# Seven half-size products for the gate projections of a two-block DiT kernel

## The chip, the cores and the metric

The kernel runs on one core of a Trainium2 chip. The metric is the device time of one execution in microseconds (us). The core has four compute engines with queues of their own: TensorE (PE, matmuls, with weight loads shown as PEld), VectorE (DVE), ScalarE (ACT) and GpSimd (POOL); SyncE (SP) here only issues DMAs. Engines meet through semaphores, and the whole order of the work is written out by hand.

## The reference

Two transformer blocks run one after the other over 256 context and 256 latent tokens, all in float32. The first part of the first block is a gated recurrence (HGRN2) with 16 heads of 128. Its projection is what the change touches:

```
def project(h):                                   # h: (tokens, 1024)
    q, i_in, f_fw, f_bw, z = jnp.split(h @ w_in, 5, axis=-1)   # w_in: 1024 x (5 * 2048)
    for d, g in enumerate((f_fw, f_bw)):
        log_f = logaddexp(log(lb), log1p(-lb) + log_sigmoid(g))  # lb is 0 for layer 0
        k = (1 - lb) * sigmoid(-g)
    return silu(q), i_in, gates, z
def readout(o, z):
    return (rmsnorm(o, o_gain) * silu(z)) @ w_out
```

With a lower bound of zero the forget gate f is sigmoid(g) and its key is sigmoid(-g). The recurrence itself runs both ways over the tokens, in chunks. After it `x = x + gate * rmsnorm(y)`, then an attention block, then the second transformer block with its feed-forward network.

## The kernel before

Activations lie with features on the partitions: `hT[:, k, t]` holds feature k*128+p of token t, with 512 columns, 256 of the context and 256 of the latents. `xT` is the residual stream in the same layout; between its normalization at the start and the end of the recurrence nobody reads or writes it.

The recurrence works through 8 pairs of heads. A **turn** of TensorE, `hg_turn_all(i)`, makes the projections of pair i and between them the core of pair i-1. There are five strips of weights a pair, each 1024 x 256, loaded into the slots of a ring by SyncE one turn ahead, in the order of `HG_ORDER = (2, 3, 0, 4, 1)`, which is f_fw, f_bw, q, z, v. A strip is used at idx = 2j and 2j+1, once for each of the two heads (m = 0, 1). `hg_project_tensor` (the matmul at L705) makes 8 matmuls of 128 x 512 for each, in PSUM bank idx % 2; a float32 matmul is two instructions in the trace, so a projection is 16 instructions of 512 columns. Strip 4 (v, L714) is made the other way round, tokens on the partitions.

Behind each projection `hg_core_after(i-1, idx)` runs a piece of the core: score matmuls of term 0 (L749) and of terms 1 to 7 (L752), at idx 7 transposes (L764), at idx 8 states (L776), at idx 9 outputs and means (L794, L800). Then `hg_mods_tensor` does part of a modulation projection for later blocks (L471) at idx 0, 2, 4 and 6.

The other engines, in the order of their own queues:

- ScalarE, for each idx: `hg_keys_scalar`, which packs the keys of the next term into K_c (L1507); then `hg_project_scalar`, which reads the projection out of PSUM: two sigmoids for f (L1489, L1490), one for q and z (L1496), a copy for v (L1498). At the end of a turn it takes squares and square roots (L1523, L1526).
- VectorE: `hg_scores_vector` for terms 0 to 7 (L1815 to L1830): it multiplies the keys and queries of the term (L1823, L1825: "merged"), copies the scores by a mask (L1828) and multiplies Tw (L1830). Between them stand two reciprocals of the pair before (L1864), its read-out (L1870, L1871) and from term 4 on the gating of q and z from PSUM (L1858, L1860). At the end come the states (L1841, L1844) and `hg_unpack_vector` (L1802 to L1807), which waits for the last outputs and sets up Qw, Kw and k_sum for the next pair ("unpacked").
- GpSimd: `move_pool`, once a turn, copies f and v (L2295, L2296: "moved").

TensorE's term t waits for K_c of that term (`kc_ready`), K_c for VectorE's product of the term before (`merged`), and that for the scores before it (`lv_full`). The first K_c of a pair waits for "unpacked".

The last pair's core runs beside the first part of the output projection (L1443). The second block's feed-forward network, further on, already uses Strassen's scheme (L1291): seven products of 4 matmuls of 256 columns a strip.

## Time and profile before

| | |
|---|---|
| median of 3 runs | 2645.95 us (2644.92 to 2647.23) |
| the profiled execution | 2646.15 us |
| its span, first to last instruction | 2644.4 us |
| mean granted TensorE clock | 0.988 |
| TensorE busy | 97% |
| VectorE, ScalarE, GpSimd busy | 40%, 22%, 7% |
| turns of the recurrence with an interleaved core | 7, from 117.8 us to 846.9 us |

A row of the timeline gives the start, the duration, the engine, the line, the operation with its output and inputs, the shapes, how many instructions are merged in the row, and in brackets the idle time before it with what ended it. A matmul row is some tenths longer than its share of the queue, since its end includes the drain; the distance from start to next start is what it costs. A wait inside a row is not shown as idle time.

### The profile page before, as it was taken

To read this page: it belongs to the slowest core of one execution; us is meant where nothing else is said; L and a number is where in the kernel's file an instruction comes from. 1 tells how busy PE (TensorE), PEld (TensorE's weight loads), DVE (VectorE), ACT (ScalarE), POOL (GpSimd) and SP (SyncE) were. 2 spreads that over 40 slices of the span, in tenths; PEclk is the share of its full clock that TensorE was granted. 3 is DMA by queue.
4 is the path that set the end of the run, shared out by engine and by line. 5 is a ranking of instruction groups with operands and counts; after the bars stand their busy time and mean duration, and the time that the engine had idled before them with its cause. 6 is when DMAs were issued, how large, how long until landed. Compare 5 with 4: busy or idle time off the path is not lost.

```text
span 2644.4 us, 31395 instructions
## 1 busy us (share of the span) xinstructions
PE 2557.8 (97%) x12728; PEld 1838.1 (70%) x12728; DVE 1067.6 (40%) x1883; ACT 574.6 (22%) x1118; POOL 175.9 (7%) x138
## 2 busy tenths in 40 slices
PE   7999999999999898899999999989999999998999
PEld 3556656656566576666886444678886587888998
DVE  2245365364464712254126111146664014115961
ACT  3112222122121112133224100121111013112211
POOL 0000000000000010000000000022120000003410
PEclk9999999999999998999999999999999999999999
DMA  8443343343424042212430122133333232344662
GB/s 314 159 159 131 124 143 111 127 159 114 140 96 112 9 142 80 70 38 71 119 94 9 59 68 63 64 96 91 84 102 88 66 80 64 104 150 129 175 170 70
DMA packets 319737, 280.58 MB, mean 106 GB/s; under 512 B 27617, under 2 KB 298601, under 8 KB 319513
## 3 DMA queue, kind: packets, MB, share of 16 engines
q1 hardware_dynamic: 317882, 274.89, 33.9%
q0 software_dynamic: 1280, 4.20, 0.4%
q8 instruction: 70, 1.15, 0.2%
q14 instruction: 26, 0.21, 0.0%
q10 hardware_dynamic: 479, 0.13, 0.0%
HBM read 278.15 MB, written 1.05 MB: 106 GB/s over the span
## 4 chain that ended last, share of the span: by engine, by line
PE 89%; DVE 7%; ACT 2%; issue 1%; DMA 1%; SPq 1%; ACTq 0%; DVEq 0%
PE ps L705 17%; PE ps L1291 11%; PE ps L1220 9%; PE ps L1363 4%; PE ps L714 4%; PE ps L1351 4%; PE ps L752 4%; PE ps L1232 3%; PE ps L1258 3%; PE ps L471 2%; PE ps L838 2%; PE ps L909 2%; PE ps L858 2%; DVE arena L2125 2%; PE ps L1064 2%; PE ps L794 1%
## 5 line engine op out<-in xcount | busy, mean ns | idle before, releaser
L705 PE MATMUL ps<-hT,ring_mem 128*128 128x512 f32 x1024 | 455.7, 598 | 1.7 <-ACT hT L484 1.7
L705 PEld LDWEIGHTS ps<-hT,ring_mem 128*128 128x128 f32 x1024 | 191.2, 191 | 234.9 <-issue 232.7
L1220 PE MATMUL ps<-hT,ring_mem 128*128 128x512 f32 (+1 forms) x768 | 250.3, 486 | 0.0
L1220 PEld LDWEIGHTS ps<-hT,ring_mem 128*128 128x128 f32 x768 | 145.9, 190 | 101.3 <-issue 91.4
L1291 PE MATMUL ps<-arena 128*128 128x256 f32 (+1 forms) x704 | 132.7, 332 | 13.8 <-DVE arena L2084 13.8
L2056 DVE TENSOR_TENSOR arena<-ps,arena 128x512 f32<-128x512 f32 (+1 forms) x48 | 26.8, 559 | 291.2 <-PE ps L1232 291.2
L752 PEld LDWEIGHTS ps<-arena,K_c 128*128 128x128 f32 x896 | 117.2, 196 | 32.6 <-issue 20.1
L1291 PE MATMUL ps<-hT,arena 128*128 128x256 f32 (+1 forms) x704 | 131.4, 330 | 0.0
L1291 PE MATMUL ps<-hT,ring_mem 128*128 128x256 f32 (+1 forms) x704 | 124.5, 330 | 4.2 <-DMA ring_mem<-in_w_up_dram 4.2
L1291 PEld LDWEIGHTS ps<-arena 128*128 128x128 f32 x704 | 111.8, 195 | 23.8 <-issue 14.3
L752 PE MATMUL ps<-arena,K_c 128*128 128x128 f32 x896 | 121.2, 290 | 7.4 <-ACT K_c L1507 7.3
L1291 PEld LDWEIGHTS ps<-hT,ring_mem 128*128 128x128 f32 x704 | 109.3, 194 | 14.1 <-DMA ring_mem<-in_w_up_dram 4.9
L423 DVE RECIPROCAL rstd<-root 128x256 f32<-128x256 f32 (+2 forms) x18 | 31.6, 1753 | 214.8 <-ACT root L396 214.8
L1351 PE MATMUL ps<-arena,ring_mem 128*128 128x512 f32 (+1 forms) x352 | 116.0, 491 | 2.1 <-DVE arena L2135 2.1
L1291 PEld LDWEIGHTS ps<-hT,arena 128*128 128x128 f32 x704 | 111.4, 194 | 9.5
L1363 PE MATMUL ps<-arena,ring_mem 128*128 128x256 f32 (+1 forms) x704 | 116.6, 327 | 0.0
L1363 PEld LDWEIGHTS ps<-arena,ring_mem 128*128 128x128 f32 x704 | 106.5, 191 | 10.1 <-issue 1.1
L714 PE MATMUL ps<-ring_mem,hT 128*128 128x256 f32 x512 | 113.0, 379 | 0.0
L2065 DVE SCALAR_TENSOR_TENSOR xT<-ps,mod_b,xT 128x256 f32<-128x256 f32 (+1 forms) x60 | 23.6, 427 | 216.2 <-PE ps L1351 88.3
L714 PEld LDWEIGHTS ps<-ring_mem,hT 128*128 128x128 f32 x512 | 96.1, 190 | 12.4
L1351 PEld LDWEIGHTS ps<-arena,ring_mem 128*128 128x128 f32 x352 | 67.7, 193 | 49.5 <-issue 41.4
L1507 ACT ACTIVATE K_c<-arena 128x1024 f32<-128x1024 f32 x56 | 64.0, 1143 | 170.9 <-DVE arena L1825 148.4
(278 smaller groups left out, 3668.0 us busy)
## 6 DMA issues: line engine op xcount, KB each, us to landing
ring_mem<-in_w_mod_dram SPq DMA_DIRECT2D x24, 2048.0 KB, 7.6
ring_mem<-in_w_up_dram SPq DMA_DIRECT2D x88, 512.0 KB, 5.2
ring_mem<-in_hg_w_in_dram SPq DMA_DIRECT2D x40, 1024.0 KB, 5.1
ring_mem<-in_w_in_dram SPq DMA_DIRECT2D x30, 1024.0 KB, 5.4
ring_mem<-in_w_down_dram SPq DMA_DIRECT2D x16, 1408.0 KB, 7.1
ring_mem<-in_ada_w_dram SPq DMA_DIRECT2D x8, 2048.0 KB, 7.7
ring_mem<-in_mla_w_in_dram SPq DMA_DIRECT2D x9, 1024.0 KB, 5.4
ring_mem<-in_hg_w_out_dram SPq DMA_DIRECT2D x8, 1024.0 KB, 12.0
```

Of the source, the lines that this page charges most:

```text
L471: mm = PE.matmul(bank[c * 32:c * 32 + 32, 0:256], sil_cols[:, cond * 16 + 2 * k:cond * 16 + 2 * k + 32], wm[:, k % 4, c * 256:c * 256 + 25 ...
L705: mm = PE.matmul(bank, wj[:, k, m * 128:m * 128 + 128], hT[:, k, :], start=k == 0, stop=k == 7)
L714: mm = PE.matmul(bank[:, g * 256:g * 256 + 256], hT[:, k, tok:tok + 128], wj[:, k, :], start=k == 0, stop=k == 7)
L752: mm = PE.matmul(dst, K_c[:, u * 128:u * 128 + 128], comb(Qw, 1 << (term - 1), u), start=True, stop=True)
L838: mm = PE.matmul(ps[:, 4 - 4 * h + j, 0:256], strip("hg_out", j, 16)[:, k, :], oz[:, k, h * 256:h * 256 + 256], start=k == 0, stop=k == 15)
L1220: mm = PE.matmul(ps[:, j, 0:n], wj[:, k, m * 128:m * 128 + 128], hT[:, k, c0:T], start=k == 0, stop=k == 7)
L1232: mm = PE.matmul(ps[:, 3 + j, 0:n], wj[:, k, m * 128:m * 128 + 128], brT[:, k, c0:T], start=k == k0, stop=k == k1 - 1)
L1258: mm = PE.matmul(ps[:, (0 if part == "_a" else 4) + j, m * (hi - lo):(m + 1) * (hi - lo)], wj[:, k, m * 128:m * 128 + 128], yT[:, k, c0 + ...
L1291: mm = PE.matmul(up_region(f, which, hw), left[:, k, :], right[:, k, 0:hw], start=k == 0, stop=k == 3)
L1351: mm = PE.matmul(ps[:, j, 0:n], wj[:, k, :], hid[:, k, 0:n], start=k == 0, stop=k == FT - 1)
L1363: mm = PE.matmul(ps[:, (4 if part == "_a" else 0) + j, 0:hi - lo], wj[:, k, :], hid[:, k, lo:hi], start=k == 0, stop=k == FT - 1)
L1507: S.activation(view(K_c, (2 * h, PC // (2 * h)), (h, 2), (1, h)), comb(Kw, h), ACT.Copy).then_inc(kc_ready, 1)
```

## The change

In turns 1 to 7 the four gate strips are no longer multiplied head by head. A strip A (1024 x 256 weights, as 2 x 2 blocks: feature half by head) and the activations B (feature half by token half) are multiplied by seven products of half the size, each 4 matmuls of 128 x 256. The first turn and the v strip stay as they were.

- Four sums of activations, T_hg, are made once, by VectorE in turn 0. They lie where xT lies. So xT is stored to a buffer in device memory first (`x_saved`), and loaded back after the last turn's fourth strip (`x_back`), ahead of the strips of the output projection; VectorE waits for it ahead of hg_post.
- Four sums of weights a strip: S1 and S3 by VectorE (`hg_sums_vector`, S3 in place), S2 and S4 by GpSimd (in place, after the products that need the old blocks).
- The seven products share the two PSUM banks 0 and 1, four regions of 256 columns, so that some have to be copied out before the next: ScalarE copies the first product of the sum P1, the seventh, the second and the fifth (`hg_one_scalar` and so on). VectorE adds them up in `hg_gather_vector`; the result ("whole") lies in SBUF.
- P1 and the two others lie over the states of the pair before (St), S1 and the whole z over its turned keys (kTw).
- The sigmoids and the gating now read the whole strip from SBUF, one strip later (`hg_signed_scalar`, `hg_read_gate_vector`, `hg_query_gate_vector`). The strips come in the order f_fw, z, q, f_bw, v.

```
-        HG_ORDER = (2, 3, 0, 4, 1)
+        HG_FIRST, HG_ORDER = (2, 3, 0, 4, 1), (2, 4, 0, 3, 1)
...
+            sp.wait_ge(x_copied, KT)
+            sp.dma_start(x_apart, xT.rearrange("p k t -> p (k t)")).then_inc(x_saved, 16)
...
+            sp.wait_ge(strips_used, (PAIRS - 1) * 5 + (hg_first + 4))
+            sp.wait_ge(x_saved, 16)
+            sp.dma_start(xT.rearrange("p k t -> p (k t)"), x_apart).then_inc(x_back, 16)
...
+        def hg_seven_tensor(pe, i, idx):
+            j, second = divmod(idx, 2)
+            a11, a12, a21, a22 = hg_parts(j)
+            one, six = ps[:, 0, 0:256], ps[:, 0, 256:512]
+            five, seven = ps[:, 1, 0:256], ps[:, 1, 256:512]
...
+            if not second:
+                ring.wait_loaded(pe, "hg_in", j, i)
+                if j == 0:
+                    pe.wait_ge(act_freed, i * 6 - 1)
+                else:
+                    pe.wait_ge(u_ready, nth(i, j - 1))
+                product(one, a11, hT[:, 0:4, 0:256]).then_inc(one_full, 1)
+                if j == 0:
+                    pe.wait_ge(act_freed, i * 6)
+                else:
+                    pe.wait_ge(whole_ready, nth(i, j - 1))
+                pe.wait_ge(s3_ready, nth(i, j))
+                product(seven, a21, T_hg[:, 2]).then_inc(seven_full, 1)
+                pe.wait_ge(one_kept, nth(i, j))
+                product(one, a12, hT[:, 4:8, 0:256]).then_inc(two_full, 1)
+                pe.wait_ge(seven_kept, nth(i, j))
+                product(seven, a22, T_hg[:, 3])
+                return
+            product(five, S1_hg, T_hg[:, 0]).then_inc(five_full, 1)
+            pe.wait_ge(two_kept, nth(i, j))
+            pe.wait_ge(s2_ready, nth(i, j))
+            product(six, a11, T_hg[:, 1]).then_inc(six_full, 1)
+            pe.wait_ge(five_kept, nth(i, j))
+            pe.wait_ge(s4_ready, nth(i, j))
+            strip_used(product(five, a12, hT[:, 4:8, 256:512]))
...
+        def hg_one_scalar(act, i, j):
+            act.wait_ge(one_full, nth(i, j))
+            if j == 0:
+                act.wait_ge(o_full, raised(i * 2 - 2))
+                act.wait_ge(unpacked, i)
+                act.wait_ge(moved, i)
+            else:
+                act.wait_ge(whole_ready, nth(i, j - 1))
+            S.activation(P1_hg, ps[:, 0, 0:256], ACT.Copy).then_inc(one_kept, 1)
...
-                    hg_project_scalar(act, i, idx)
+                    j = idx // 2
+                    if idx >= 8:
+                        hg_project_scalar(act, i, idx)
+                    elif idx % 2:
+                        hg_five_scalar(act, i, j)
+                    else:
+                        hg_one_scalar(act, i, j)
+                        if j:
+                            hg_signed_scalar(act, i, j - 1)
+                        hg_seven_scalar(act, i, j)
+                        hg_two_scalar(act, i, j)
                     if idx == 7:
+                        act.wait_ge(dve_freed, i * 4 + 2)
                         hg_turn_scalar(act, i - 1)
+                        hg_signed_scalar(act, i, 3)
...
+        def hg_gather_vector(dve, st, i, j):
+            dve.wait_ge(one_kept, nth(i, j))
+            dve.wait_ge(two_kept, nth(i, j))
+            V.tensor_tensor(hg_part(j, 0, 256), hg_part(j, 0, 256), P1_hg, ALU.add)
+            dve.wait_ge(six_full, nth(i, j))
+            V.tensor_tensor(P1_hg, P1_hg, ps[:, 0, 256:512], ALU.add).then_inc(u_ready, 1)
+            dve.wait_ge(u_ready, nth(i, j))
+            dve.wait_ge(seven_kept, nth(i, j))
+            dve.wait_ge(five_kept, nth(i, j))
+            st.link(V.tensor_tensor(hg_part(j, 256, 512).rearrange("p (s t) -> p s t", s=2), view(P1_hg, (0, 2), (1, 256)),
+                                    P57_hg.rearrange("p (s t) -> p s t", s=2), ALU.add))
+            st.mark(V.tensor_tensor(hg_part(j, 768, 256), hg_part(j, 512, 256), P57_hg[:, 0:256], ALU.add))
+            dve.wait_ge(strips_used, ring.stages["hg_in"]["first"] + i * 5 + (j + 1))
+            st.settle()
+            V.tensor_tensor(hg_part(j, 256, 512), hg_part(j, 256, 512), ps[:, 1, :], ALU.add).then_inc(whole_ready, 1)
+            if j < 3:
+                hg_sums_vector(dve, st, i, j + 1)
...
+                    if gates and term % 2:
+                        hg_gather_vector(dve, st, i + 1, term // 2)
...
             with pool.Fori(1, PAIRS) as i:
+                for j in range(4):
+                    a11, a12, _, _ = hg_parts(j)
+                    pool.wait_ge(s3_ready, nth(i, j))
+                    pool.wait_ge(one_kept, nth(i, j))
+                    nc.gpsimd.tensor_tensor(a11, S1_hg, a11, ALU.subtract).then_inc(s2_ready, 1)
+                    pool.wait_ge(two_kept, nth(i, j))
+                    pool.wait_ge(s2_ready, nth(i, j))
+                    nc.gpsimd.tensor_tensor(a12, a12, a11, ALU.subtract).then_inc(s4_ready, 1)
                 move_pool(pool, i)
```

How TensorE's queue reads at the start of a turn. A matmul here is one row entry where the trace has two instructions. Before (L705 the projection, L749 and L752 scores):

```order
L705 MATMUL ps<-hT,ring_mem 128x512 x8
L740 ISA
L749 MATMUL ps<-arena 128x128 x8
L742 ISA
L745 ISA
L752 MATMUL ps<-arena,K_c 128x128 x4
```

And now, with the waits of each (L721 a product, L816 and L819 scores):

```order
L721 MATMUL ps<-hT,ring_mem 128x256 [waits act_freed]
L721 MATMUL ps<-hT,ring_mem 128x256 x3
L734 ISA [waits act_freed]
L721 MATMUL ps<-xT,ring_mem 128x256 [waits s3_ready]
L721 MATMUL ps<-xT,ring_mem 128x256 x3
L721 MATMUL ps<-hT,ring_mem 128x256 [waits one_kept]
L721 MATMUL ps<-hT,ring_mem 128x256 x3
L721 MATMUL ps<-xT,ring_mem 128x256 [waits seven_kept]
L721 MATMUL ps<-xT,ring_mem 128x256 x3
L807 ISA [waits unpacked]
L816 MATMUL ps<-arena 128x128 [waits rt_ready]
```

The wait on one_kept stands in the middle of the first strip, ahead of all scores, where before nothing stood between the strip's start and its end.

ScalarE's queue at the start of a turn, before (L1507 K_c, L1489 and L1490 the sigmoids of f):

```order
L1507 ACT_TABLE_LOAD
L1507 ACTIVATE K_c<-arena 128x1024 [waits unpacked]
L726 ISA
L1489 ACT_TABLE_LOAD [waits moved,unpacked]
L1489 ACTIVATE arena<-ps 128x512 [waits proj_full]
L1490 ACTIVATE arena<-ps 128x512
```

And now (L1622 K_c, L1585 the copy of the first product, L1589 of the seventh, L1595 of the second, L1604 and L1606 the sigmoids of f over the whole strip):

```order
L1622 ACT_TABLE_LOAD
L1622 ACTIVATE K_c<-arena 128x1024 [waits unpacked]
...
L1585 ACTIVATE arena<-ps 128x256 [waits moved,unpacked,o_full]
L1589 ACTIVATE arena<-ps 128x256 [waits seven_full]
L1595 ACTIVATE arena<-ps 128x256 [waits two_full]
...
L1622 ACTIVATE K_c<-arena 128x1024 [waits merged]
L1585 ACTIVATE arena<-ps 128x256 [waits whole_ready,one_full]
L1604 ACT_TABLE_LOAD
L1604 ACTIVATE arena<-arena 128x1024 [waits whole_ready]
...
L1606 ACTIVATE arena<-arena 128x1024 [waits act_freed]
L1589 ACTIVATE arena<-ps 128x256 [waits seven_full]
```

The table load and the sigmoids of strip 0 have moved into strip 1, between the copy of its first product and that of its seventh.

## Rows read from the trace of the kernel before

**Rows 1.** The page, busy time by engine and the chain that ended last.
```profile
PE 2557.8 (97%) x12728; PEld 1838.1 (70%) x12728; DVE 1067.6 (40%) x1883; ACT 574.6 (22%) x1118; POOL 175.9 (7%) x138
...
PE 89%; DVE 7%; ACT 2%; issue 1%; DMA 1%; SPq 1%; ACTq 0%; DVEq 0%
```
**Rows 2.** Timeline of TensorE in two steady turns: start, duration, line, operation.
```profile
221.97 7.03 PE L705 MATMUL ps<-hT,ring_mem 128*128 128x512 f32 x16
...
326.12 7.03 PE L705 MATMUL ps<-hT,ring_mem 128*128 128x512 f32 x16
332.98 1.95 PE L749 MATMUL ps<-arena 128*128 128x128 f32 x16
334.82 2.92 PE L752 MATMUL ps<-arena,K_c 128*128 128x128 f32 x16
337.67 1.93 PE L471 MATMUL ps<-ring_mem,sil_cols 128*32 128x256 f32 x32
339.53 7.13 PE L705 MATMUL ps<-hT,ring_mem 128*128 128x512 f32 x16
346.50 2.08 PE L752 MATMUL ps<-arena,K_c 128*128 128x128 f32 x16
```
**Rows 3.** Timeline of TensorE in the feed-forward stage, the starts of two strips, one after the other.
```profile
1810.83 3.62 PE L1291 MATMUL ps<-hT,ring_mem 128*128 128x256 f32 x16
...
1822.92 3.62 PE L1291 MATMUL ps<-hT,ring_mem 128*128 128x256 f32 x16
```
**Rows 4.** Timeline of VectorE at the start of the turn of 326.12.
```profile
324.68 2.29 DVE L1802 TENSOR_TENSOR arena<-arena 128x2048 f32<-128x2048 f32 x1 [9.96 <-PE ps L794]
...
337.77 2.22 DVE L1825 TENSOR_TENSOR arena<-arena 128x1024 f32<-128x1024 f32 x1
...
342.41 3.35 DVE L1864 RECIPROCAL root<-root 128x512 f32<-128x512 f32 x1
345.68 1.16 DVE L1823 TENSOR_TENSOR arena<-arena 128x1024 f32<-128x1024 f32 x1
```
**Rows 5.** Timeline of ScalarE at the start of the same turn.
```profile
331.87 1.51 ACT L1507 ACTIVATE K_c<-arena 128x1024 f32<-128x1024 f32 x1 [2.90 <-DVE arena L1807]
333.40 1.28 ACT L1489 ACT_TABLE_LOAD   x1
334.69 0.60 ACT L1489 ACTIVATE arena<-ps 128x512 f32<-128x512 f32 x1
...
349.88 1.06 ACT L1507 ACTIVATE K_c<-arena 128x1024 f32<-128x1024 f32 x1 [2.10 <-DVE arena L1825]
```
**Rows 6.** Timeline of all engines in the feed-forward stage, one strip.
```profile
1847.90 0.69 DVE L2143 TENSOR_TENSOR arena<-ring_mem 128x512 f32<-128x512 f32 x1
1848.50 0.41 DVE L2108 TENSOR_TENSOR arena<-root,ps 128x256 f32<-128x256 f32 x1
1848.73 1.27 POOL L2334 TENSOR_TENSOR arena<-arena,ring_mem 128x512 f32<-128x512 f32 x1 [9.45 <-DVE arena L2143]
...
1859.38 0.39 ACT L1706 ACTIVATE root<-ps 128x256 f32<-128x256 f32 x1 [2.09 <-PE ps L1291]
```
**Rows 7.** Timeline of TensorE in the last pair's core, rows behind gaps.
```profile
868.71 3.49 PE L752 MATMUL ps<-arena,K_c 128*128 128x128 f32 x16 [2.07 <-ACT K_c L1507]
...
876.53 2.05 PE L752 MATMUL ps<-arena,K_c 128*128 128x128 f32 x16 [0.70 <-ACT K_c L1507]
...
883.45 2.05 PE L752 MATMUL ps<-arena,K_c 128*128 128x128 f32 x16 [1.44 <-ACT K_c L1507]
```
**Rows 8.** Windows there: stretch, length, TensorE's busy time, granted clock, DMA share, GB/s.
```profile
869.00:872.00 3.00, 3.00 (x17) 0.51 0.00 0
```
**Rows 9.** Timeline of VectorE in turn 0.
```profile
79.89 0.69 DVE L1858 TENSOR_TENSOR arena<-ps,arena 128x512 f32<-128x512 f32 x1 [43.52 <-ACT arena L1496]
```
**Rows 10.** The page, DMA issues: count, size, median time to landing.
```profile
ring_mem<-in_w_mod_dram SPq DMA_DIRECT2D x24, 2048.0 KB, 7.6
```
**Rows 11.** Timeline of SyncE's issues at the last turn's end.
```profile
815.17 11.71 SPq L130 DMA_DIRECT2D ring_mem<-in_hg_w_out_dram  x4
```

More of the change, by code:

```diff
@@ L167, in build @@
         xT = sb("xT", KT * T).rearrange("p (k t) -> p k t", k=KT)
+        T_hg = xT.rearrange("p k t -> p (k t)").rearrange("p (s k t) -> p s k t", s=4, k=4)
+        x_apart = nc.dram_tensor("x_apart", (128, KT * T), F32, kind="Internal").ap()
         hT = sb("hT", KT * T).rearrange("p (k t) -> p k t", k=KT)
@@ L543, in strip_load @@
             def strip_load(i, j):
-                sp.dma_start(strip("hg_in", j, 8), wk["hg_w_in"][0][:, :, bass.ds(i * 256 + HG_ORDER[j] * 2048, 256)]
+                order = HG_FIRST if isinstance(i, int) and i == 0 else HG_ORDER
+                sp.dma_start(strip("hg_in", j, 8), wk["hg_w_in"][0][:, :, bass.ds(i * 256 + order[j] * 2048, 256)]
                              ).then_inc(loaded[j], 16)
@@ L680, in hg_mods_tensor, with nth, hg_parts, product @@
                 mod_turn_tensor(pe, mod_number(i, s_), mod_bank(s_))
+        def nth(i, j):
+            return i * 4 + (j - 3)
+        def hg_parts(j):
+            wj = strip("hg_in", j, 8)
+            return wj[:, 0:4, 0:128], wj[:, 4:8, 0:128], wj[:, 0:4, 128:256], wj[:, 4:8, 128:256]
+        def hg_seven_tensor(pe, i, idx):
[3 more added lines that the diff above has]
+            five, seven = ps[:, 1, 0:256], ps[:, 1, 256:512]
+            def product(dst, left, right):
+                for k in range(4):
+                    mm = PE.matmul(dst, left[:, k, :], right[:, k, :], start=k == 0, stop=k == 3)
+                return mm
+            if not second:
[23 more added lines that the diff above has]
+            strip_used(product(five, a12, hT[:, 4:8, 256:512]))
         def hg_project_tensor(pe, i, idx):
@@ L1498, in hg_project_scalar, with hg_part, hg_seven_scalar, hg_two_scalar @@
                 S.activation(v_st[:, 2 * m:2 * m + 2, :], bank, ACT.Copy).then_inc(act_freed, 1)
+        hg_whole = (f_st[:, 1, :], z_hg, q_st, f_st[:, 0, :])
+        def hg_part(j, at, n):
+            return hg_whole[j][:, at:at + n]
+        def hg_one_scalar(act, i, j):
[4 more added lines that the diff above has]
+                act.wait_ge(moved, i)
+            else:
+                act.wait_ge(whole_ready, nth(i, j - 1))
+            S.activation(P1_hg, ps[:, 0, 0:256], ACT.Copy).then_inc(one_kept, 1)
+        def hg_seven_scalar(act, i, j):
+            act.wait_ge(seven_full, nth(i, j))
+            S.activation(P57_hg[:, 256:512], ps[:, 1, 256:512], ACT.Copy).then_inc(seven_kept, 1)
+        def hg_two_scalar(act, i, j):
+            act.wait_ge(two_full, nth(i, j))
+            if j == 2:
+                act.wait_ge(lv_full, i * 16 - 14)
+            S.activation(hg_part(j, 0, 256), ps[:, 0, 0:256], ACT.Copy).then_inc(two_kept, 1)
+        def hg_five_scalar(act, i, j):
+            act.wait_ge(five_full, nth(i, j))
+            S.activation(P57_hg[:, 0:256], ps[:, 1, 0:256], ACT.Copy).then_inc(five_kept, 1)
+        def hg_signed_scalar(act, i, j):
+            act.wait_ge(whole_ready, nth(i, j))
+            if j in (0, 3):
+                S.activation(k_st[:, 1 - j // 3, :], hg_whole[j], ACT.Sigmoid, scale=-1.0).then_inc(act_freed, 1)
+                act.wait_ge(act_freed, i * 6 + (2 * (j // 3) + 1))
+                S.activation(hg_whole[j], hg_whole[j], ACT.Sigmoid).then_inc(act_freed, 1)
+                return
+            if j == 1:
+                act.wait_ge(o_ready, raised(i * 2 - 2))
+            for m in range(2):
+                if j == 2:
+                    act.wait_ge(dve_freed, i * 4 + (m + 1))
+                S.activation(sg[:, m, :], hg_part(j, m * T, T), ACT.Sigmoid).then_inc(sig_ready, 1)
         def hg_keys_scalar(act, i, term):
@@ L2202, in _ @@
             modulate_coef(st, mod_a[0][:, 8:16, :], vecs[:, PRE:PRE + 8])
+            hg_turned_vector(dve)
             for idx in range(4, 8):
@@ L2208, in _, with core @@
             hg_unpack_vector(dve, st, 0)
-            def core(i, gates, first=False):
+            hg_sums_vector(dve, st, 1, 0)
+            def core(i, gates, first=False, more=True):
                 hg_scores_vector(dve, st, i, 0)
@@ L2217, in core @@
                         hg_read_vector(dve, st, i - 1)
+                    if gates and term % 2:
+                        hg_gather_vector(dve, st, i + 1, term // 2)
                     if gates and term == 4:
                         hg_mods_vector(dve, i + 1, 0)
-                    if gates and term >= 4:
-                        hg_gate_vector(dve, i + 1, term)
+                        for m in range(2):
+                            hg_read_gate_vector(dve, i + 1, m)
+                    if gates and term == 6:
+                        for m in range(2):
+                            hg_query_gate_vector(dve, i + 1, m)
                 if gates:
@@ L2225, in core @@
                 if gates:
+                    if more:
+                        hg_sums_vector(dve, st, i + 2, 0)
                     hg_unpack_vector(dve, st, i + 1)
             core(0, True, True)
-            with st.loop(2, PAIRS - 1, LEVELS + 4) as i:
+            with st.loop(2, PAIRS - 1, LEVELS + 16) as i:
                 core(i - 1, True)
-            core(PAIRS - 2, True)
+            core(PAIRS - 2, True, more=False)
             core(PAIRS - 1, False)
```

64 lines of the change are left out of this document (50 added, 14 removed).

## The prediction

> **What bounds the kernel now.** I read the page's busy line and chain first. TensorE is busy for 97% of the span and holds 89% of the chain that ended last, VectorE 7% [rows 1]. So work taken from TensorE counts in full, as long as nothing makes it wait. Then I took one steady turn of the head-pair loop on TensorE's timeline [rows 2]: the same projection matmul starts at 221.97 and at 326.12, so a turn is 104.15 us. Its instructions stand end to end, and the weight strips are there in time. The reader should see in these rows what the seven-microsecond first projection does: while it runs, VectorE unpacks the last pair and ScalarE makes the first K_c. Last I read those two engines at the start of the turn [rows 4, 5], the stage of this same kernel that already runs Strassen products [rows 3, 6], and the rows after TensorE's longer gaps [rows 7, 8].
>
> The profiled execution took 2646.15 us (span 2644.4 and 1.75 around it), 0.2 us above the median of 2645.95, so I work from 2646.15. No change that this kernel's measurement can tell is under about 0.2% (5.3 us).
>
> **What is removed.** In turns 1 to 7 each of four strips has two projections of 16 instructions of 512 columns. One takes 6.97 us from start to next start after the modulation matmuls (339.53 to 346.50) and 6.87 after scores (the next at 348.42 runs so); together 13.84 us [rows 2]. Seven products take 12.09 us a strip in the feed-forward stage (1810.83 to 1822.92) and so 1.73 each, weight loads hidden [rows 3]. The saving is 1.75 a strip, 7.0 a turn, 49 over seven turns. Taken alone that gives 2597.
>
> **What the first strip of a turn waits for.** I set the start of the turn to 0, which is 326.12. Before, ScalarE read the first projection only at 7.1, so its needs were met. Now the third product waits for one_kept, ScalarE's copy of the first product. That copy stands behind three things: unpacking by VectorE, the v and f move by GpSimd, and, in ScalarE's own queue, the first K_c. Unpacking starts when the last outputs are done, at -1.44 (324.68) [rows 4], and ends at 5.7; K_c runs from 5.75 to 7.26 (331.87, 1.51 long) [rows 5]. The copy adds 0.39 (a copy of 256 columns in the stage with Strassen) [rows 6]. TensorE has two products before it, to 3.45, and can go on at about 7.7. That is a new gap of 4.2 us, in each of turns 2 to 7, since nothing in this chain is made shorter. In turn 1 unpacking is long done and the move and first K_c set the end; I take 0.7 there.
>
> **What the second strip waits for.** The remaining two products run to 11.15. Scores 0 and 1 take 1.84 and 2.85 (332.98 to 334.82 to 337.67 [rows 2]), and end at 15.85. VectorE's step of term 1 then follows: the Q product ends 2.3 later (2.22 long, 337.77), the masked copies and the product on Tw take 2.4 to the start of a reciprocal at 342.41, and that 3.35 [rows 4]. It is then 24.0. Only behind these does its gather of strip 0 stand: three adds of 0.41 and one of 0.69, then the 0.69 that reads the last products, then 0.69 twice for the weight sums of strip 1 [rows 6]. With the handovers it is ready at 27.9. TensorE is through mods, three products, scores 2 and the next strip's first product at 26.5: a gap of 1.4. Then the copy of the first product stands on ScalarE behind K_c for term 3, which needs term 2 merged by VectorE (about 1.2 for each of two products after the sums [rows 4], then 1.06 for K_c [rows 5] and 0.39): copy done at 31.6, TensorE there at 29.7, a gap of 1.9. Next ScalarE has the sigmoids of the finished strip ahead of the copy of the seventh product, two of 1024 elements at about 1.0 each, and the table load of 1.28 that used to stand at the turn's start [rows 5] and now stands here. Copy done at 35.2, TensorE at 33.4: 1.8 to 1.9. The same bookkeeping for strips 2 and 3 gives 1.1 (a queue of hg_read and the gather on VectorE, with K_c 5 behind) and 0.6 (K_c 7). Together 7.0 in strips 1 to 3.
>
> So a steady turn gets 4.2 + 7.0 = 11.2 of waits for 7.0 of products: +4.2. Turn 1 has no reciprocals and no unpacking in the way; its waits come to 4.1, so it is 2.9 shorter. Over the stage: 6 x 4.15 - 2.9 = +22.
>
> **What a gap costs besides itself.** After a gap of 2.07 us that ended at 868.71 the granted clock fell to 0.51 in 869 to 872 [rows 7, 8], the lower of the two levels (1.2 GHz): 16 instructions took 3.49 instead of the 2.05 that the same ones take after a gap of 0.70 [rows 7], and the stretch of 3 us and some tenths at half speed is worth 1.5 to 1.7 us. The gap of 4.2 is twice as long, with as little in front of it as two products, so I count 1.7 for each of six turns: +10. For the gaps of 1.4, 1.9 and 1.9 I count nothing more: a slower product there mostly eats the wait for ScalarE that follows it; the upper end takes another 1.7 a turn. The Trainium skill ("TensorE: Matmul & The Clock Gate", "HAM oscillation — how this bites in real kernels") says that a loop whose short bursts are broken by waits falls back to the half clock in every turn, and the trace agrees at this gap; by that rule the case to reckon with is the one where the second strip's gaps do it too.
>
> **The other edits.** VectorE gets 5 adds and 2 sums a strip, 3.4 us, 13.7 a turn; it is 40% busy [rows 1], and this costs only where it is named above. Four sums of 1024 elements in turn 0, about 1.2 each, stand in an idle time of 43.5 us before 79.89 [rows 9]; the store of 2 MB they wait for takes about the 7.6 us of a load of that size [rows 10] and is issued near 42: nothing, and if it took 30 us more, still nothing. GpSimd's two differences a strip (1.27 beside VectorE's adds, which stay at 0.41 [rows 6]) have the scores and modulation matmuls, about 5 us, as cover: nothing; at twice the time still nothing. VectorE's sums for the next turn's first strip lie in its idle time before unpacking (9.96 us [rows 4]). The load back and, behind it, the strips of the output projection start 20 us later than before (815.17 [rows 11]), about 25 us before their first use; 7.6 and some 12 us for them fit. If not, up to 5 us, once. Against all this the lower bound of the waits is the 4.2 gap alone (its chain has a row for each step); the other 7.0 rest on laying the three queues beside each other, and I bound them by 2 and 12 a turn.
>
> The table load is the other place where page and row differ. The row shows 1.28 and the next activation 1.29 after it started [rows 5]. The Trainium skill ("ScalarE: Activation LUTs", "What ACT_TABLE_LOAD costs") counts a drain besides, 2.66 us together; by it the third gap of strip 1 would be 1.4 longer and the sum, as an estimate from that page, 8 us higher. I keep the row.
>
> Sum: 2646 + 22 + 10 = 2678.
>
> **The rivals.**
> *Only the first gap counts.* If VectorE and ScalarE stay ahead in strips 1 to 3 (it needs the gather to come before TensorE's second product of the next strip, thus 1.4 us found, and K_c 3 earlier by 1.9), a turn is 7.0 - 4.2 - 1.7 = 1.1 shorter, turn 1 6.3: 2646 - 13 = 2633. For it: VectorE idles half of the turn. Against: its work of terms 1 and 2 is packed, with both reciprocals and slow strided products. It turns to slower where the waits of strips 1 to 3 pass 1.1 a turn. Chance 0.09.
> *Clock falls twice a turn.* The second strip's gaps bring the clock down as well, with a cost that reaches the five products behind them, or the 4.2 gap brings two slow stretches: 1.7 more in each of six or seven turns, 2690. For: three gaps with 1.73 of work between them. Against: a gap of 1.44 left the 2.05 of the matmuls behind it as it was [rows 7]. Chance 0.22.
> *The gaps leave the clock alone* and the waits are as laid: 2668. Against it stands what followed the gap of 2.07 [rows 7, 8]. Chance 0.12.
> *The products don't come at 1.73*, as weights now come from sums in place: the same kind of operand runs at 1.73 in the other stage [rows 3], so 0.02; about 2690.
> *Net nothing*: waits smaller by a third: 2646 to 2655. Chance 0.07.
> The forecast, the waits as laid and one slow stretch a turn, has the remaining 0.48; its own range is 2667 to 2688. The range for 8 in 10 is 2652 to 2698. Faster by over 0.2%: 0.09. Within 0.2%: 0.05. Slower: 0.86.
>
> **What would show it.** On TensorE a steady turn of about 110 us, with a gap of about 4 us, released by ScalarE's copy of 256 columns, after two products; the granted clock at 0.5 right behind it. Gaps of 1 to 2 us in strip 1, released by VectorE's subtraction on ring_mem and by ScalarE's copies, the latter behind a table load. The first turn near 101 to 102. Products at 1.73. No idle time at the first output strips and none before hg_post. I am wrong if steady turns come below 104, if the largest gap is not the one at the turn's start, or if GpSimd's differences release TensorE.

## The result, and the profile after

| | before | after |
|---|---|---|
| median of 4 runs each, us | 2646.38 (2644.92 to 2647.23) | 2685.13 (2683.56 to 2687.28) |
| ratio after / before | | 1.0149, 95% interval 1.0133 to 1.0164 |
| the profiled execution: time, span, us | 2646.15, 2644.4 | 2683.56, 2681.8 |
| mean granted clock of TensorE | 0.988 | 0.983 |

The change makes the kernel 39 us slower. The forecast was 2678, its own range 2667 to 2688.

The page of the kernel after, busy time and the chain that ended last, to be laid beside [rows 1]:
```profile
PE 2533.0 (94%) x13400; PEld 1969.3 (73%) x13400; DVE 1194.6 (45%) x2083; ACT 607.3 (23%) x1202; POOL 266.1 (10%) x194
...
PE 74%; DVE 14%; issue 9%; ACT 3%; DMA 0%; DVEq 0%; POOL 0%; ACTq 0%; SPq 0%; POOLq 0%
```
TensorE is busy for 25 us less, and the span is 37 us longer, so it stands idle for some 62 us more. Its share of the chain that ended last falls from 89% to 74%. VectorE's rises from 7% to 14%, and that of "issue", time in which an engine waited for nothing that the profile shows, from 1% to 9%.

What TensorE waits for from 100 to 880 us, after (waiting tensor and line, releaser, us in total, times, longest):
```profile
PE ps L721 <- ACT arena L1585: 44.3, 28, 4.0
PE ps L721 <- ACT arena L1589: 12.1, 7, 1.7
PE ps L721 <- DVE ring_mem L1996: 6.3, 6, 1.1
PE ps L831 <- ACT arena L1633: 1.8, 7, 0.3
```
L721 is the product of the new projections. L1585 is ScalarE's copy of the first product, L1589 that of the seventh, L1996 VectorE's sum of weights. Before, only the last row's wait was there in these turns (2.1 in all). The sum of the first three is 62.7 us in 41 waits.

TensorE's timeline after, one steady turn's first strips and the next turn's start (start, duration, line, operation, in brackets the idle time before and its releaser); it answers [rows 2]:
```profile
330.31 1.89 PE L721 MATMUL ps<-hT,ring_mem 128*128 128x256 f32 x8
332.04 1.89 PE L721 MATMUL ps<-xT,ring_mem 128*128 128x256 f32 x8
337.90 3.78 PE L721 MATMUL ps<-hT,ring_mem 128*128 128x256 f32 x8 [3.97 <-ACT arena L1585]
341.47 2.74 PE L721 MATMUL ps<-xT,ring_mem 128*128 128x256 f32 x8
344.05 1.95 PE L816 MATMUL ps<-arena 128*128 128x128 f32 x16
...
360.74 1.99 PE L721 MATMUL ps<-xT,ring_mem 128*128 128x256 f32 x8 [1.05 <-DVE ring_mem L1996]
364.37 1.99 PE L721 MATMUL ps<-hT,ring_mem 128*128 128x256 f32 x8 [1.64 <-ACT arena L1585]
368.10 1.99 PE L721 MATMUL ps<-xT,ring_mem 128*128 128x256 f32 x8 [1.73 <-ACT arena L1589]
...
385.52 1.99 PE L721 MATMUL ps<-hT,ring_mem 128*128 128x256 f32 x8 [0.95 <-ACT arena L1585]
...
404.10 1.99 PE L721 MATMUL ps<-hT,ring_mem 128*128 128x256 f32 x8 [0.59 <-ACT arena L1585]
...
441.95 1.89 PE L721 MATMUL ps<-hT,ring_mem 128*128 128x256 f32 x8
```
Product follows product at 1.73 (330.31 to 332.04), as in the stage that had them before [rows 3]. This turn takes 111.64, against 104.15. The seven turns start at 117.45, 219.84, 330.31, 441.95, 552.4, 663.9 and 775.98, and the last ends at 886.62: 102.39, then 110.5, 111.6, 110.4, 111.5, 112.1 and 110.6.

The windows at the end of the first gap of that turn and behind it (stretch, length, busy time, granted clock, DMA share, GB/s), for [rows 8]:
```profile
337.00:338.00 1.00, 0.10 (x1) 0.50 0.00 0
338.00:342.00 4.00, 4.00 (x10) 0.50 0.00 0
342.00:344.00 2.00, 2.00 (x8) 0.71 0.00 0
344.00:356.00 12.00, 12.00 (x91) 1.00 0.34 113
```
The clock falls while TensorE still stands idle (1.00 from 334 to 336, 0.67 from 336 to 337), is at its lower level, 1.2 GHz, when the copy is done, and stays there for some 5 us behind the gap of 3.97. The two products there take 3.57 and 2.58 from start to start instead of 1.83 and 1.73: 2.6 us lost.

Why the copy is late is seen on VectorE and ScalarE, as in [rows 4, 5]. VectorE's timeline after, at the turn's start:
```profile
328.87 2.29 DVE L1929 TENSOR_TENSOR arena<-arena 128x2048 f32<-128x2048 f32 x1 [8.62 <-PE ps L861]
...
334.83 1.21 DVE L1934 TENSOR_TENSOR arena<-arena 128x1024 f32<-128x1024 f32 x1
...
353.49 3.35 DVE L2038 RECIPROCAL root<-root 128x512 f32<-128x512 f32 x1
...
359.99 0.69 DVE L1996 TENSOR_TENSOR ring_mem<-ring_mem 128x512 f32<-128x512 f32 x1
```
ScalarE's timeline in the same stretch:
```profile
336.07 1.50 ACT L1622 ACTIVATE K_c<-arena 128x1024 f32<-128x1024 f32 x1 [2.90 <-DVE arena L1934]
337.48 0.37 ACT L1585 ACTIVATE arena<-ps 128x256 f32<-128x256 f32 x1
...
362.99 1.06 ACT L1622 ACTIVATE K_c<-arena 128x1024 f32<-128x1024 f32 x1 [9.98 <-DVE arena L1952]
363.95 0.37 ACT L1585 ACTIVATE arena<-ps 128x256 f32<-128x256 f32 x1
364.33 1.28 ACT L1604 ACT_TABLE_LOAD   x1
365.63 1.06 ACT L1604 ACTIVATE arena<-arena 128x1024 f32<-128x1024 f32 x1
...
367.68 0.36 ACT L1589 ACTIVATE arena<-ps 128x256 f32<-128x256 f32 x1
```
Each copy that TensorE needs takes 0.37 and stands behind something long that doesn't concern it: at 337.48 behind the unpacking and the first K_c, at 363.95 behind K_c of term 3, at 367.68 behind a table load and two sigmoids. VectorE's sum of weights (359.99) stands behind the gather, and that behind a reciprocal of 3.35.

Part of the unpacking ahead of 337.48 is long because two engines copy at once. At 118.31, with VectorE idle, GpSimd's two copies of the move take 1.89 and 1.04, and at 107.25, with GpSimd idle, VectorE's two copies of the unpacking take 0.69 each. In this turn both run together from 328.88 on: VectorE's take 2.38 and 1.52, GpSimd's 4.03 and 1.50. So some 2.5 us of the chain ahead of the first K_c come with this overlap. It is there in the kernel before too, where the first projection covers it; no run here took it away.

### The profile page after: what moved, and what is told of

It is laid out like the page before. It is cut to its first block, busy times and chain, and to the rows that moved or that the text cites. A ratio compares the mean times of both kernels' runs of the same rounds, so it can differ in the third digit from the quotient of the medians.

```text
span 2681.8 us, 33406 instructions
## 1 busy us (share of the span) xinstructions
PE 2533.0 (94%) x13400; PEld 1969.3 (73%) x13400; DVE 1194.6 (45%) x2083; ACT 607.3 (23%) x1202; POOL 266.1 (10%) x194
## 4 chain that ended last, share of the span: by engine, by line
PE 74%; DVE 14%; issue 9%; ACT 3%; DMA 0%; DVEq 0%; POOL 0%; ACTq 0%; SPq 0%; POOLq 0%
PE ps L1358 11%; PE ps L1287 9%; PE ps L721 7%; PE ps L1430 4%; PE ps L1418 4%; PE ps L781 4%; PE ps L1299 3%; PE ps L1325 3%; PE ps L905 2%; PE ps L976 2%; PE ps L925 2%; DVE arena L1952 2%; PE ps L819 2%; DVE arena L2299 2%; PE ps L1131 2%
## 5 line engine op out<-in xcount | busy, mean ns | idle before, releaser
L1287 PEld LDWEIGHTS ps<-hT,ring_mem 128*128 128x128 f32 x768 | 145.9, 190 | 101.3 <-issue 91.4
L721 PE MATMUL ps<-hT,ring_mem 128*128 128x256 f32 x672 | 171.7, 401 | 44.3 <-ACT arena L1585 44.3
L721 PEld LDWEIGHTS ps<-hT,ring_mem 128*128 128x128 f32 x672 | 130.2, 200 | 75.3 <-ACT arena L1585 55.6
L721 PE MATMUL ps<-xT,ring_mem 128*128 128x256 f32 x672 | 163.0, 386 | 18.5 <-ACT arena L1589 12.1
L721 PEld LDWEIGHTS ps<-xT,ring_mem 128*128 128x128 f32 x672 | 129.3, 194 | 41.7 <-ACT arena L1589 15.0
L1358 PE MATMUL ps<-arena 128*128 128x256 f32 (+1 forms) x704 | 132.7, 332 | 13.9 <-DVE arena L2258 13.9
L1622 ACT ACTIVATE K_c<-arena 128x1024 f32<-128x1024 f32 x56 | 64.0, 1143 | 353.9 <-DVE arena L1952 331.3
L819 PE MATMUL ps<-arena,K_c 128*128 128x128 f32 x896 | 119.0, 287 | 7.4 <-ACT K_c L1622 7.3
L819 PEld LDWEIGHTS ps<-arena,K_c 128*128 128x128 f32 x896 | 115.1, 192 | 14.6 <-ACT K_c L1622 11.7
L1358 PEld LDWEIGHTS ps<-hT,ring_mem 128*128 128x128 f32 x704 | 109.2, 193 | 13.8 <-DMA ring_mem<-in_w_up_dram 4.5
L1430 PEld LDWEIGHTS ps<-arena,ring_mem 128*128 128x128 f32 x704 | 106.5, 191 | 10.1 <-issue 1.1
## 6 DMA issues: line engine op xcount, KB each, us to landing
ring_mem<-in_hg_w_out_dram SPq DMA_DIRECT2D x8, 1024.0 KB, 12.1
```

What stands on the lines that cost most here:

```text
L721: mm = PE.matmul(dst, left[:, k, :], right[:, k, :], start=k == 0, stop=k == 3)
L819: mm = PE.matmul(dst, K_c[:, u * 128:u * 128 + 128], comb(Qw, 1 << (term - 1), u), start=True, stop=True)
L1287: mm = PE.matmul(ps[:, j, 0:n], wj[:, k, m * 128:m * 128 + 128], hT[:, k, c0:T], start=k == 0, stop=k == 7)
L1358: mm = PE.matmul(up_region(f, which, hw), left[:, k, :], right[:, k, 0:hw], start=k == 0, stop=k == 3)
L1430: mm = PE.matmul(ps[:, (4 if part == "_a" else 0) + j, 0:hi - lo], wj[:, k, :], hid[:, k, lo:hi], start=k == 0, stop=k == FT - 1)
L1622: S.activation(view(K_c, (2 * h, PC // (2 * h)), (h, 2), (1, h)), comb(Kw, h), ACT.Copy).then_inc(kc_ready, 1)
```

## The experiments

In all of them names are those of the kernel after. An edit can move the line numbers by a few: the second sum of weights, L1996, is L2000, L2001 or L2005 in some runs, and the copy of the first product, L1585, is L1588 in one. A ratio is to the kernel before, run on the same chip in the same set (its medians there 2645.1 to 2645.5).

**One part alone: the products.** The kernel before with its two projections of a strip in turns 1 to 7 made as seven products of 4 x 256 columns, with no sums, differences, copies or extra waits; part of the gate projections is left out by that.
```
-            for n ... k in range(8): matmul over 512 columns      (two projections, 32 instructions)
+            for n in range(4 - m):                                 (m = 0, 1: 4 + 3 products)
+                for k in range(4):
+                    mm = PE.matmul(bank[:, n % 2 * 256:n % 2 * 256 + 256], wj[...], hT[...], start=k == 0, stop=k == 3)
```


> The kernel before, with each projection of turns 1 to 7 made of 4 (first head) or 3 (second head) products of 4 matmuls of 256 columns in place of 8 of 512; no sums, no copies, no store of the residual stream. It leaves out part of the gate projections. It is the price of the seven products with nothing to wait for. My theory: 12.09 us a strip instead of 13.84, 49 us less in all, 2597 (2594 to 2601). Rival (weight loads of 0.19 us show beside matmuls of 0.22, or the shorter projections uncover waits for K_c): 2610 or more.

Measured: 2597.01, ratio 0.9817 (0.9801 to 0.9834). The prediction's first term alone gave 2597. Of the 48 us some 46 are in the turns, which take 97.56 against 104.15, so 6.6 a turn instead of 7.0. The rest lies in the last pair's core, 63.8 us long against 65.5, where the clock fell at other places. So the whole 88 us between 2597 and 2685 is what the scheme costs around its products.

**One part alone: the residual stream's trip to memory.** The kernel before plus the store of xT, VectorE's wait for it, the load back and the wait for that.
```
+            sp.dma_start(x_apart, xT.rearrange("p k t -> p (k t)")).then_inc(x_saved, 16)
...
+            dve.wait_ge(x_saved, 16)
...
+            sp.dma_start(xT.rearrange("p k t -> p (k t)"), x_apart).then_inc(x_back, 16)
...
+            dve.wait_ge(x_back, 16)
```


> The kernel before with only the store of the residual stream to device memory after its fourth strip load, the wait of VectorE for it in turn 0, the load back ahead of the output projection's strips, and VectorE's wait for that; nothing writes over xT. My theory: nobody waits for either, within 0.1% of the kernel before, 2643 to 2649. Rival (2 MB ahead of the output projection's strips make TensorE wait at its first use): 2650 or more.

Measured: 2644.48, ratio 1.0001 (0.9992 to 1.001). It costs nothing that can be measured. What the products lose is lost within the turns.

**The first gap taken away.** Strip 0's first and fifth product are kept in sg, which is free then, and no longer in the buffer that unpacking fills. So both copies can go ahead of the first K_c, and the waits for unpacking and the move go to the copy of the second product.
```
-        P1_hg, P57_hg = St_flat[:, 0:256], St_flat[:, 256:768]
+        P1_of = lambda j: sg_flat[:, 0:256] if j == 0 else St_flat[:, 0:256]
...
-                act.wait_ge(unpacked, i)         (in hg_one_scalar, j == 0)
+                act.wait_ge(dve_freed, i * 4)
...
+                    if idx == 0:                 (ahead of hg_keys_scalar)
+                        hg_one_scalar(act, i, 0)
+                        hg_seven_scalar(act, i, 0)
```


> The changed kernel, with the products of strip 0 kept in sg, which is idle then, so that ScalarE copies the first and the seventh product at once and ahead of the first K_c; only the copy of the second product waits for unpacking. My theory (the gap at a turn's start is the chain unpacking, K_c, copy, and it costs a slow stretch of the clock besides): the gap of 4.1 us (start 332.04 to 337.90 less a product) and 1.6 us of slow clock go in six turns, 0.7 in the first, nothing comes back: steady turns of 105.5 to 106 instead of 111.5, 2649 us in all (2643 to 2656). Rival (VectorE, packed with terms 1 and 2, sets the pace, and the time comes back as longer gaps in strip 1): above 2670.

Measured: 2645.73, ratio 1.0001 (0.9991 to 1.001); turns of 104.9 to 105.0. TensorE's timeline at the turn's start has no gap and no slow product:
```profile
326.60 1.89 PE L723 MATMUL ps<-hT,ring_mem 128*128 128x256 f32 x8
328.32 1.89 PE L723 MATMUL ps<-xT,ring_mem 128*128 128x256 f32 x8
...
346.94 1.99 PE L723 MATMUL ps<-xT,ring_mem 128*128 128x256 f32 x8 [1.11 <-DVE ring_mem L2005]
350.57 1.99 PE L723 MATMUL ps<-hT,ring_mem 128*128 128x256 f32 x8 [1.64 <-ACT arena L1585]
354.30 1.99 PE L723 MATMUL ps<-xT,ring_mem 128*128 128x256 f32 x8 [1.74 <-ACT arena L1589]
```
The first gap was worth 39 us. The turns are 6.2 shorter than the kernel after's 111.1 (the mean of turns 2 to 7), of which the gap's idle time is 4.0, its restart 0.26 (below), and the rest, some 2.0, fits the slow clock, which is gone from behind it. The edit changes the buffer and the order of the copies at once, so it doesn't say which of the two would have been enough. The other waits stayed as they were, and by themselves they eat the whole saving of the products.

**The waits of strips 1 to 3 taken away.** There both copies go ahead of the term's K_c, and the sigmoids go last. Strip 0 stays as in the kernel after.
```
+                    if idx in (2, 4, 6):         (ahead of hg_keys_scalar)
+                        hg_one_scalar(act, i, j)
+                        hg_seven_scalar(act, i, j)
...
                         hg_two_scalar(act, i, j)
+                        if j:
+                            hg_signed_scalar(act, i, j - 1)
```


> The changed kernel, with ScalarE's copies of the first and seventh product of strips 1 to 3 ahead of K_c, and the sigmoids of the finished strip last of the idx. The gap at the turn's start stays. My theory (the gaps in strips 1 to 3 come from the order in ScalarE's queue): of the gaps of strip 1 only the one that VectorE's sums end (1.05) is left, and about 0.8 before strip 2's second product; 5.5 us a steady turn, 3.5 in the first: 2649 (2642 to 2657). Rival (K_c, now later, holds up the scores by as much): 2670 or above.

Measured: 2656.16, ratio 1.0042 (1.0026 to 1.0059), 29 us below the kernel after. That misses my 2649, though it is inside the range given: a steady turn is 4.0 us shorter (107.1 against 111.1), not 5.5, and the first one 3.9. TensorE's timeline shows what stayed and what came:
```profile
331.14 3.45 PE L721 MATMUL ps<-hT,ring_mem 128*128 128x256 f32 x8 [3.97 <-ACT arena L1585]
...
365.79 1.99 PE L721 MATMUL ps<-hT,ring_mem 128*128 128x256 f32 x8 [0.20 <-ACT arena L1599]
...
372.84 1.99 PE L721 MATMUL ps<-xT,ring_mem 128*128 128x256 f32 x8 [1.18 <-DVE ring_mem L2000]
```
Three waits for L1585 and one for L1589 are gone from each turn, and a new one for VectorE's sum has come in the third strip (12 such waits, 13.6 us over the stage, against 6 and 6.3). L1599, the copy of the fifth product, holds it up by 0.2. TensorE, arriving earlier, finds the next late engine.

**Only the sigmoids moved.** The table load and the sigmoids go behind the copies, while K_c stays ahead of them.
```
                         hg_one_scalar(act, i, j)
-                        if j:
-                            hg_signed_scalar(act, i, j - 1)
                         hg_seven_scalar(act, i, j)
                         hg_two_scalar(act, i, j)
+                        if j:
+                            hg_signed_scalar(act, i, j - 1)
```


> The changed kernel, with ScalarE's sigmoids of the finished strip, and the table load ahead of them, behind the copies of the seventh and second product; K_c stays ahead of the first copy. My theory: the gap of 1.74 before strip 1's fourth product goes and nothing else: 1.9 to 2.0 in each of seven turns, 2671 (2666 to 2676). Rival (the sigmoids, later, hold up the copy of the fifth product or the gating): 2680 or more.

Measured: 2668.12, ratio 1.0092 (1.0077 to 1.0107), 17 us below the kernel after. What TensorE waits for from 100 to 870 us:
```profile
PE ps L721 <- ACT arena L1585: 44.3, 28, 4.0
PE ps L721 <- DVE ring_mem L1996: 6.4, 6, 1.1
...
```
The row of L1589 is gone, the others are as they were. That row was 12.1 us in 7 waits; with 0.26 for each restart (below) it is worth 13.9, or 2.0 a turn. The steady turns are shorter by 1.9 (109.3 against 111.1). In the profiled executions the seven turns together are 13.2 shorter (755.98 against 769.17), which the wait and its restart cover. The other 3 us of the 17 lie elsewhere: the kernel before was itself 1.3 faster in this set (2645.08 against 2646.38), and the stretch behind the last turn, which the edit doesn't touch, takes from 1791.5 to 1798.1 in the profiled executions of all these kernels.

**Strip 1's gaps as one chain.** The gather of strip 0 goes ahead of the first reciprocal, in VectorE's order. If gaps add up one by one, 1.05 of 9.9 goes and the kernel gets faster. If the reciprocal only moves ahead of term 2, K_c 3 comes later instead.
```
+                    if gates and term == 1:
+                        hg_gather_vector(dve, st, i + 1, 0)
...
-                    if gates and term % 2:
+                    if gates and term in (3, 5, 7):
```


> The changed kernel, with VectorE's first reciprocal of a turn behind the gather of strip 0 instead of ahead of it. My theory (the three gaps of strip 1 are one chain: VectorE's queue up to merged of term 2, then K_c, then the copy): the gap of 1.05 that VectorE's sums end goes, but merged of term 2 comes 0.8 later since VectorE now idles for the strip's last product before its gather, so the gap before the third product grows by 1.05 + 0.26 + 0.5 or so; a steady turn 0.3 to 0.8 longer, 2688 (2684 to 2692). Rival (each gap has its own cause and taking one away gains it): 1.3 less a turn, 2677.

Measured: 2691.55, ratio 1.018 (1.0166 to 1.0194): slower than the kernel after by 6 us, by 8 if the ratios are compared. A steady turn is 1.6 longer (112.7 against 111.1), where 0.3 to 0.8 was expected. Its VectorE and then its TensorE:
```profile
357.73 0.69 DVE L1996 TENSOR_TENSOR ring_mem<-ring_mem 128x512 f32<-128x512 f32 x1
358.34 3.35 DVE L2038 RECIPROCAL root<-root 128x512 f32<-128x512 f32 x1
```
```profile
359.76 1.89 PE L721 MATMUL ps<-xT,ring_mem 128*128 128x256 f32 x8
365.31 3.78 PE L721 MATMUL ps<-hT,ring_mem 128*128 128x256 f32 x8 [3.66 <-ACT arena L1585]
369.04 3.03 PE L721 MATMUL ps<-xT,ring_mem 128*128 128x256 f32 x8
```
The sum of weights is in time (359.76 follows with no idle). The gap of 1.05 is now part of the next one, which grows from 1.64 to 3.66, and behind that the products run at half speed: 3.73 and 2.86 from start to start. The slow products also cover the wait for L1589, which is gone from the steady turns. A turn has 0.8 less idle time and 0.5 less for two restarts, and 2.9 more for the slow products (3.73 and 2.7 to 2.9 instead of 1.83 and 1.73), a term that the expectation didn't have. So the gap that was closed came back in the next one, in the same chain from the end of scores 1 to K_c 3, and one long gap cost more here than two short ones, since the clock fell.

**What the clock costs.** Two products that nobody reads, of the same operands as the third, go between the second and third product of strip 0, into a free bank. They do 3.45 us of useless work in the 4 us gap, and in turn 1, where the gap is 0.67, they are mostly extra work.
```
+                if j == 0:
+                    for _ in range(2):
+                        product(ps[:, 2, 0:256], a12, hT[:, 4:8, 0:256])
```


> The changed kernel with two useless products of 4 matmuls of 256 columns (3.45 us of work whose result nobody reads, in PSUM bank 2) at the start of each turn, between the first two products and the wait for the copy. More work in the same gap. My theory (a gap costs the wait and a slow stretch of the clock behind it): the idle time falls from 4.0 to about 0.5 in six turns, the granted clock stays up there, each steady turn is about 1.6 us shorter, the first turn 2.8 longer: about 7 us less than the changed kernel, 2678 (2674 to 2682). Rival (the slow matmuls behind the gap, 3.4 to 3.6 for 1.83, come from the wait itself or from the operands): as the changed kernel or 3 us more, 2685 to 2688.

Measured: 2675.02, ratio 1.0115 (1.01 to 1.0131). With more work, the kernel is 10 us faster than the kernel after (9 by the ratios).
```profile
334.41 3.62 PE L721 MATMUL ps<-hT,ring_mem 128*128 128x256 f32 x16
338.54 1.99 PE L721 MATMUL ps<-hT,ring_mem 128*128 128x256 f32 x8 [0.52 <-ACT arena L1588]
340.37 1.89 PE L721 MATMUL ps<-xT,ring_mem 128*128 128x256 f32 x8
```
From the turn's first product (330.95) to the third product's start it is 7.59, to the hundredth what the kernel after shows (330.31 to 337.90). So the copy comes when it did, and what changed is the speed behind it: 1.83 and 1.73 for the two products, with a granted clock of 1.00 from 335 to 344. The six steady turns are 2.1 shorter each (109.0 against 111.1), and the first is 2.5 longer (104.9 against 102.4); together that is the 10 us. So the slow clock cost 2.1 a steady turn, more than the 1.6 expected and the 1.7 of the prediction.

The Trainium skill ("TensorE: Matmul & The Clock Gate", "HAM oscillation — how this bites in real kernels") tells of short bursts of matmuls, each followed by a wait for a DMA, after each of which the clock is down again. The waits here are for another engine's copy. The clock was down behind each of the six first gaps of 3.8 to 4.0 us, and behind none of the gaps of strip 1.

**All together.** The two orders of copies, and the last pair's read behind the gather of strip 1 instead of ahead of it.
```
-                    if idx in (2, 4, 6):
+                    if idx in (0, 2, 4, 6):      (copies ahead of K_c in every strip)
...
-                    if not first and term == 3:
-                        hg_read_vector(dve, st, i - 1)
                     if gates and term % 2:
                         hg_gather_vector(dve, st, i + 1, term // 2)
+                    if not first and term == 3:
+                        hg_read_vector(dve, st, i - 1)
```


> Both edits of e1 and e2 together, and VectorE's read-out of the last pair after the gather of strip 1. My theory: of the waits of a turn only the 1.05 before strip 1's second product is left, a steady turn of about 99.5 to 100: 2646 less 49 for the products plus about 10 for what is left = 2607 (2600 to 2614), below the kernel before. Rival (VectorE's longer queue, 66 us of work a turn, becomes the bound once TensorE's waits are gone): 2625 or more.

Measured: 2611.08 (2608.62 to 2613.43), ratio 0.9868 (0.9852 to 0.9885); turns of 100.4. This version beats both kernels: 35 us faster than before, 74 faster than after. From the expectation's 2607 it is 4 off. What TensorE still waits for, from 200 to 800 us, in this run (the copies of the fifth product are L1603 here):
```profile
PE ps L723 <- DVE ring_mem L2001: 6.7, 6, 1.2
PE ps L821 <- ACT K_c L1626: 4.0, 6, 0.7
...
PE ps L723 <- ACT arena L1603: 0.9, 5, 0.2
```
The first is the sum of weights behind the reciprocal, the second K_c. With 0.26 for each of 17 restarts the three rows make 16.0 in six turns, 2.7 a turn; the turn is 2.8 above the 97.56 of the products alone. The moved read was not run alone, so its share is not known.

## Why the prediction was right

*The saving.* 1.73 a product: right. Worked out 7.0 a turn, measured 6.6 (products alone): the product behind the modulation matmuls takes 1.83 up to the next start, as the projection there took 6.97 instead of 6.87. I had left that 0.10 out of the new side.

*The gap at the turn's start.* Predicted 4.2, with a restart at 7.7 from the turn's start. Measured: a restart at 7.59, 4.13 after the point where the third product would have begun (two of 1.73). The cause, a copy behind unpacking and the first K_c, was right, and taking it away brought back 39 us. In turn 1, 0.7 was predicted and 0.67 is there.

*Strips 1 to 3.* Predicted 1.4, 1.9, 1.8 to 1.9, 1.1 and 0.6, each with its releaser. From start to start they are 1.21, 1.80, 1.89, 1.11 and 0.75, with those releasers (the idle rows plus 0.16, next point): 6.8, against 7.0.

*What a wait costs beside its idle row.* A product starts 1.73 after the one before, but its record is 1.89 long; idle time is counted from the record's end, so it leaves out 0.16. The product behind a wait then takes 1.83 up to the next start. Together 0.26 a wait, 10.6 over 41 waits. My terms, made from start to start, held the 0.16 and not the 0.10, which is 4 us over the 41 waits.

*The clock.* Predicted 1.7 for each of six turns, from the rows behind another gap [rows 7, 8]. That it falls was right; the size was low. Behind the first gap of turns 2 to 7 the two products lose 1.6, 2.6, 1.4, 2.5, 3.0 and 1.6, in all 12.7 or 2.1 a turn. The first of them:
```profile
227.25 3.60 PE L721 MATMUL ps<-hT,ring_mem 128*128 128x256 f32 x8 [3.80 <-ACT arena L1585]
230.69 1.89 PE L721 MATMUL ps<-xT,ring_mem 128*128 128x256 f32 x8
```
(230.69 - 227.25 is 3.44, less 1.83.) Filling the gap gave the same 2.1 a steady turn. The rival with a second fall in each turn did not come: behind the gaps of strip 1 the products take 1.99. Its total of 2690 is nearer to the measured 2685 than the forecast, but by a mechanism that the rows don't show. Where one gap there was made 3.66 long, in the run with the gather ahead, the clock did fall.

*The sum.* The turn from 330.31 to 441.95: -6.6 for products, +9.9 idle, +1.6 for six restarts, +2.6 for the clock, together +7.5, and 111.64 - 104.15 is 7.5. Turn 1: -6.6 + 3.6 idle + 1.3 for five restarts is -1.7, and 102.39 - 104.15 is -1.8. All seven turns are 40 us longer (769.2 against 729.1), where the prediction had 32 (22 for waits and products, 10 for the clock): the products saved 3 less, the 0.10 of the restarts makes 4, the clock nearly 3, and the gaps were laid 2 too long. In the rest of the kernel the profiled execution is 2.7 faster, mostly in the last core, and its 2683.56 is 1.6 below the median. That makes the forecast 7 low.

*The other edits at nothing.* Right for the store and load (2644.48 with them alone). GpSimd's differences release TensorE nowhere in the table of waits, though they are not free for VectorE: its multiply at 368.58 takes 2.16 beside one of them (368.39), where the same one took 1.16 before, and it stays off TensorE's path. The five adds and two sums of a strip, counted at 3.4 us for this term and at some 3.9 in the laying of strip 1, run from 356.76 to 360.60, 3.84. The load back starts 25.1 us before the output projection's first use, as predicted (before, its strips had 31.7, so "20 us later" doesn't fit the 25), and the strips behind it are in time: their first product has no idle ahead of it:
```profile
861.50 0.35 SPq L598 DMA_DIRECT2D xT<-x_apart  x1
```
```profile
886.62 3.60 PE L1515 MATMUL ps<-arena,ring_mem 128*128 128x512 f32 x8
```

*The table load.* The row rules, as chosen. At 364.33 the load takes 1.28 and the sigmoid starts 1.30 after it, directly behind a copy that ended at 364.3. The 2.66 that the Trainium skill gives ("ScalarE: Activation LUTs", "What ACT_TABLE_LOAD costs") would have made the third gap 1.4 longer; it is 1.73. As this wait is in turn 1 too, the page's figure would have added an estimated 10 us to the sum, not 8.

What stays open: how the 88 us divide to better than a few microseconds, and what the overlap of the two engines' copies at the turn's start is worth. The single removals don't add up to the joint one: without the first gap 39 us, and without most of the waits of strips 1 to 3 another 29, come to 68, and both together with the moved read gave 74.

## What to carry to other kernels

Splitting a product into more and smaller ones with results that must be copied out gives every other engine's order a say in TensorE's time. Before making such a change, write down for each copy what stands ahead of it in its engine's queue and which buffer it waits for: here the arithmetic saved 49 us, the queues as they stood took 88, and three reorderings with one other buffer gave 74 of them back. Count a wait as its idle row plus 0.26, add about 2 where the clock falls, as it did behind each gap of 3.6 us and more in these turns and behind none of 1.8 or less, and treat short gaps in a row as one chain: closing one that isn't the last to be late only moves it.

## What the hardware showed that was not expected

Useless work in a gap made the kernel faster by 10 us, with the same restart time to the hundredth in the turn shown.

The clock's answer to a gap is not fixed by the gap. In the last core of the kernel before, a gap of 2.07 was followed by 3.49 at half speed [rows 7]; in the same place after, the gap is 2.06 and the fall comes later, mostly in the matmuls after it:
```profile
908.41 2.56 PE L819 MATMUL ps<-arena,K_c 128*128 128x128 f32 x16 [2.06 <-ACT K_c L1622]
910.76 4.81 PE L1515 MATMUL ps<-arena,ring_mem 128*128 128x512 f32 x8
...
932.09 2.05 PE L819 MATMUL ps<-arena,K_c 128*128 128x128 f32 x16 [2.41 <-ACT K_c L1622]
```
Behind the gap of 2.41 nothing is slow at all. A price of the clock read from one row is good to about a microsecond, not better: behind one and the same gap of 3.97 the kernel after paid 1.4 in one turn and 3.0 in another.
